# Indexed additions that wait once a head, four buffers for the activations on their way back, and attention steps placed ahead of the weight split

## The chip, the cores and the metric

The kernel is one program on 1 core of a Trainium2 chip. The metric is device time in microseconds (us): the median of several executions, lower is better. Engines are named as in the profile: PE is the matrix engine, DVE the vector engine, ACT the scalar engine, POOL the GpSimd engine, SP the engine whose queue loads the weights.

## The reference

The reference is a forward pass over 256 tokens of width 2048 in float32, in two blocks. Cut to what matters here:

```
# first block
proj  = rmsnorm(x) @ w_in                       # 2048 -> 6160
mixed = forgetting attention (16 heads) | dilated attention (16 heads)
h     = x + norm(mixed) @ w_out
q     = rmsnorm(h) @ w_query                    # 8 heads x 2 halves x 128
scores[h, half] = q @ sub_keys                  # 128 keys each
# per token and head: the best 16 of 16 x 16 sums -> 16 experts of 16384
gates   = softmax(best 16 sums)
h      += sum over (gates * gelu(expert_down[e] . x)) * expert_up[e]
# second block
proj  = rmsnorm(h) @ w_in_2                     # 2048 -> 5136
mixed = window attention (12 heads) | gated linear attention | stick-breaking attention (8 heads)
h    += norm(mixed) @ w_out_2
h    += relu(rmsnorm(h) @ w1)**2 @ w2           # 2048 -> 8192 -> 2048
out   = rmsnorm(h)
```

Within one head the 16 chosen experts of a token are 16 different ones. Two different heads can choose the same expert for one token; then their gates add up.

## The kernel before

**Weights.** Every large product goes through the weights in chunks of 256 rows by 512 columns (440 or 428 in the two `w_in` products), 8 chunks to a block of columns. For each chunk SP loads `raw`, ACT copies it to `w_hi` (line 558), DVE makes `w_lo = raw - w_hi` (line 563), and PE multiplies: 12 matmuls a chunk, high by high, high by low and low by high for two row tiles and two token tiles (lines 1618 to 1620, or 1769 to 1771 in the parts whose order is written out by hand). `raw`, `w_hi` and `w_lo` have 4 buffers each (`RING`), so ACT can start the split of chunk q when PE is through with chunk q-4.

**Order.** Each engine runs its own program, and semaphores join them. The programs of ACT, DVE and PE count the same chunks. Between chunks they carry the rest of the work at fixed positions: `SEQ` and `SEQ2` list the chunks of the two attention blocks, `PAIR_AT`, `SWA_AT` and `SB_AT` the chunk s = at behind which PE starts a pair of heads, and since splits run ahead, ACT and DVE have the matching step at s = at + `LEAD` (4) and later. Within a position of ACT or DVE the order is that of the text: the split of chunk s first, then the steps.

A pair of window heads on DVE and ACT: `copy_pair` (ACT, line 679), `max_swa` (DVE, lines 1463 to 1469), `exp_swa` (ACT, lines 917 to 919), `copy_swa_p` (DVE, line 1487), `out_swa` (DVE, line 1478). On PE: `turn_swa` (line 2024), the scores (line 2038), `turn_pair_p` (line 1739), `pv_swa`. The stick-breaking pairs have `copy_sb` (ACT, line 929), `sb_front`, `sb_logs` (line 1510), the addition, the weights (line 1577) and `sb_out` on DVE, and on PE the scores (line 2076), `sums_sb` (line 2087) and `pv_sb` (line 2100).

**The expert part.** All 16384 experts are computed for all tokens: 8 down rounds of 4 blocks make the hidden values, 8 up rounds multiply the gated hidden values by `expert_up`. A block's hidden values (512 experts by 256 tokens) are spilled by ACT to `hid_rows` in memory, and are brought back in the up rounds. In the first 4 down rounds DVE also searches the best 16 of each head (`search`); each of its 8 searches ends in line 1275 and releases 32 slots of one half of the tokens.

**The gates.** POOL adds each gate into a table in memory with an indexed DMA (`scatter`, line 466): one for each of the 128 slots of each of the two token halves, 256 in all, 128 elements each. A slot's addition waits until the one before it on the same table has landed:

```python
if slot:
    pool.wait_ge(added_gate[t], 16 * slot)
```

The two tables take turns, the second 16 slots behind the first. When both tables are complete, POOL loads a block's gates into `gat`, 2 buffers (line 530).

**The way back.** ACT's queue loads the hidden values of one block into `back`, one buffer (`reload`, line 771); PE transposes them (`turn_back`, line 1876); DVE multiplies by the gates (`fill`, line 1286); ACT and DVE split the product (`split_gated`, line 775; `rest`, line 1291). Four such blocks feed an up round. The steps lie at the last chunks of the block before it and the first chunks of its own first block: the first `fill` of all stands behind the split of chunk 5 of the last down block.

Of the kernel before, what the change touches and what calls it, by code (L numbers as in the profile page):

```python
# [26 lines left out]
P = 128  # L27
# [9 lines left out]
SUB = 8  # L37
# [126 lines left out]
def build(nc, a, out):  # L164

    ctx = ExitStack()
    with ctx:
# [45 lines left out]
        gat = big[:, 0:2048].rearrange("p (i t n) -> p i t n", i=2, t=NT)  # L213
# [96 lines left out]
        spilled, reloaded = sem("spilled"), sem("reloaded")  # L310
# [23 lines left out]
        gates_loaded = [sem(f"gates_loaded{i}") for i in range(2)]  # L334
# [110 lines left out]
        def _(pool):  # L445
# [16 lines left out]
            def scatter(t, slot):  # L462

                if slot:
                    pool.wait_ge(added_gate[t], 16 * slot)
                nc.gpsimd.indirect_dma_start(  # L466
                    tables[t], bass.IndirectOffsetOnAxis(ap=slot_at[:, t, slot:slot + 1].bitcast(U32), axis=0),
                    slot_gate[:, t, slot:slot + 1], None, compute_op=ALU.add).then_inc(added_gate[t], 16)
# [54 lines left out]
            for t in range(NT):  # L523
                pool.wait_ge(added_gate[t], 16 * P)
            for n in range(4 * PEER_ROUNDS):
                if n >= 2:
                    pool.wait_ge(hid_full, n - 1)
                for t in range(NT):
                    rows = tables[t].rearrange("(b p n) o -> b p (n o)", b=32, p=P)
                    pool.dma_start(gat[:, n % 2, t], rows[n]).then_inc(gates_loaded[n % 2], 16)  # L530
# [37 lines left out]
        def _(act):  # L568
# [134 lines left out]
            for s, (name, b, c) in enumerate(SEQ):  # L703
                if s == 15:
                    drain_in1(0)
                if s > 15 and s % SUB == 3 and s - 11 < 112:
                    drain_in1((s - 11) // SUB)
                if s in (157, 165, 173):
                    drain_query((s - 157) // SUB)
                split_hi(act, s // SUB, s % SUB, widths.get(name, WIDE))  # L710
                for j, at in enumerate(XTURN_AT):
                    if s == (j if j < 8 else at + LEAD):
                        x_hi_tiles(j)
                if 8 <= s < 12:
                    square_quarter(0, s - 8)
                if s == 13:
                    root(0)
                if s == 16:
                    act.wait_ge(fix_loaded, 16)
                    act.activation(ident_b[:], ident, ACT.Copy).then_inc(masks_made, 1)  # L720
                if s == 17:
                    act.wait_ge(rel_made, 1)
                    act.activation(relrow, ps[0:SWA_H, 6, 0:TW + 1], ACT.Copy).then_inc(row_copied, 1)
                if s == 22:
                    act.wait_ge(gate_abs, 1)
                    step(act.activation(fg[:, 2], fg[:, 1], ACT.Exp, scale=-1.0))
                    act.activation(fg[:, 3], fg[:, 2], ACT.Ln, bias=1.0).then_inc(gate_soft, 1)
                if s == 26:
                    act.wait_ge(cum_made, 1)
                    act.activation(c8, ps[0:16, 7, 0:S], ACT.Copy, scale=8.0).then_inc(cum_copied, 1)  # L730
                for n, at in enumerate(PAIR_AT):
                    if s == at + LEAD:
                        copy_pair(n)
                    if s == at + LEAD + 1:
                        exp_pair(n)
                if s in (94, 95):
                    square_half(1, s - 94)
                if s == 97:
# [28 lines left out]
            def reload(n):  # L767
                act.wait_ge(spilled, 16 * (n + 1))
                if not static(n) or n > 0:
                    act.wait_ge(hid_turned, n)  # L770
                act.dma_start(back[:].rearrange("p t n -> p (t n)"), hid_rows[n]).then_inc(reloaded, 16)

# [5 lines left out]
            def phase(up, nd, nu, prev_up, fill_next, extra=None, more=True):  # L778
                for i in range(4):
                    for c in range(SUB):  # L780
# [12 lines left out]
                        if i == 3 and fill_next:  # L793
                            f = 4 * (nu + 1 if up else nu)
                            if c == 5:
                                reload(f + 1)
                            if c == 6:
                                split_gated(f, (0, 4))
                            if c == 7:
                                reload(f + 2)  # L800
                        if i == 0 and up:
                            f = 4 * nu
                            if c == 0:
                                split_gated(f + 1, (1, 6))
                            if c == 1:
                                reload(f + 3)
                            if c == 2:
                                split_gated(f + 2, (2, 4))
                            if c == 3 and more:
                                reload(f + 4)  # L810
                            if c == 4:
                                split_gated(f + 3, (3, 6))
# [16 lines left out]
            def first_gates(pos):  # L829
                if pos == 20:  # L830
                    reload(0)

# [4 lines left out]
            phase(False, PEER_ROUNDS - 1, 0, False, True, first_gates)  # L837
# [21 lines left out]
            phase(True, 8, 7, True, False, open2, more=False)  # L859
# [78 lines left out]
            for s, (name, b, c) in enumerate(SEQ2):  # L938
                if s == 18:
                    drain_in2(0)  # L940
                if s >= 19 and s % SUB == 3 and s < 100:
                    drain_in2((s - 11) // SUB)
                split_hi(act, b2 + s // SUB, s % SUB, widths.get(name, WIDE))
# [20 lines left out]
                for n, at in enumerate(SWA_AT):  # L964
                    if s == at + LEAD:
                        copy_pair(PAIRS + n)
                    if s == at + LEAD + 1:
                        exp_swa(n)
                for n, at in enumerate(SB_AT):
                    if s == at + LEAD:  # L970
                        copy_sb(n)
# [29 lines left out]
        def _(dve):  # L1001
# [160 lines left out]
            for s, (name, b, c) in enumerate(SEQ):  # L1162
# [3 lines left out]
                split_lo(dve, s // SUB, s % SUB, widths.get(name, WIDE))  # L1166
                for n, at in enumerate(PAIR_AT):
                    if s == at + LEAD + 1:
                        max_pair(n)
                for j, at in enumerate(XTURN_AT):  # L1170
                    if s == (j if j < 8 else at + LEAD):
                        x_lo_tiles(j)
# [22 lines left out]
                for n, at in enumerate(PAIR_AT):  # L1195
                    if s == at + LEAD + 3:
                        copy_pair_p(n)
                    if s == at + LEAD + 5:
                        out_pair(n)
# [80 lines left out]
            def fill(f, g):  # L1280

                dve.wait_ge(gates_loaded[g % 2], 32 * (2 * f + g // 2 + 1))
# [3 lines left out]
                V.tensor_tensor(pair, pair, gat[:, g % 2].rearrange("p t (j s) -> p j t s", j=JJ), ALU.mult).then_inc(hid_full, 1)  # L1286
# [234 lines left out]
            for s, (name, b, c) in enumerate(SEQ2):  # L1521
# [44 lines left out]
                for n, at in enumerate(SWA_AT):  # L1566
                    if s == at + LEAD + 3:
                        copy_swa_p(n)
                    if s == at + LEAD + 5:
                        out_swa(n)  # L1570
                for n, at in enumerate(SB_AT):
                    if s == at + LEAD + 5:
                        dve.wait_ge(sb_sum, n + 1)
                        V.tensor_tensor(sbb, ps[:, 4:6, 0:3 * P], sbb, ALU.add).then_inc(sb_add, 1)
                    if s == at + LEAD + 7:
                        dve.wait_ge(sb_exp, n + 1)
                        V.tensor_tensor(diagonals(sbw), diagonals(sbw), strict, ALU.mult).then_inc(sb_w, 1)
                    if s == at + LEAD + 8:
                        sb_out(n)
# [26 lines left out]
        def _(pe):  # L1606
# [260 lines left out]
            def turn_back(n, g):  # L1867

                pe.wait_ge(reloaded, 16 * (n + 1))
# [4 lines left out]
                for jj in range(4):  # L1874
                    for t in range(NT):
                        last = pe.transpose(ps[:, 4 + 2 * (g % 2) + jj // 2, (jj % 2) * S + t * P:(jj % 2) * S + t * P + P],  # L1876
                                            back[:, t, jj * P:jj * P + P], ident)
                last.then_inc(hid_turned, 1)

            def phase(up, nd, nu, prev_up, fill_next, extra=None):  # L1880
                for i in range(4):
# [6 lines left out]
                    for c in range(SUB):  # L1888
# [3 lines left out]
                        if i == 3 and fill_next and c % 2:  # L1892
                            turn_back(4 * (nu + 1 if up else nu) + c // 2, c // 2)
# [305 lines left out]
```

## Time and profile before

| | us |
|---|---|
| median of 3 runs | 3235.41 |
| lowest, highest | 3235.39, 3250.27 |
| the profiled execution, its own time | 3242.3 |
| its span, first to last instruction | 3240.2 |

The profile is one execution. The span is what the trace covers; the execution's own time is 2.1 us longer. A group's "idle before" is the idle time of its engine just ahead of it, and the arrow names what ended it. Since matmuls are pipelined, the trace shows a busy PE also where each matmul only waits for the one before it to drain.

### The profile page before, as it was taken

What the parts mean: (1) busy time and instruction counts of PE and PEld (TensorE: products, weight loads), DVE (VectorE), ACT (ScalarE), POOL (GpSimd) and SP (SyncE); (2) the same over time, 40 slices, a digit from 0 to 9 for tenths busy, and PEclk for the clock granted to TensorE, in tenths of its full rate; (3) what the DMA queues carried; (4) which work ended last, traced back from release to release, by engine and by line L of the source; (5) the groups of instructions that cost most, each with busy time, mean ns of one, the idle gap of its engine ahead of it and who ended that gap; (6) DMA issues with size and microseconds to landing.
All of it is one profiled execution on the core that took longest, in us unless ns stands there. A gap on an engine that the chain in (4) does not pass through costs nothing.

```text
span 3240.2 us, 40579 instructions
## 1 busy us (share of the span) xinstructions
PE 3089.4 (95%) x14724; PEld 2614.1 (81%) x14724; DVE 1775.5 (55%) x2339; ACT 1465.0 (45%) x1822; POOL 584.5 (18%) x423
## 2 busy tenths in 40 slices
PE   8999999999999995299999999999889999999998
PEld 7988888888888884288888887899777888888886
DVE  5445564798844442255556555555657554545444
ACT  5445454555444442144344443554455544435453
POOL 3110000147777776300000000000000000000000
PEclk9999999999999998699999999999999999999999
DMA  6764467677777775477677776664345666666664
GB/s 213 241 200 133 129 215 258 183 218 210 223 223 215 215 220 124 123 227 221 217 231 235 237 233 220 188 204 136 109 126 152 192 191 189 188 193 184 191 187 151
DMA packets 215975, 627.60 MB, mean 194 GB/s; under 512 B 58139, under 2 KB 58789, under 8 KB 215472
## 3 DMA queue, kind: packets, MB, share of 16 engines
q1 hardware_dynamic: 156544, 549.79, 54.9%
q0 software_dynamic: 49856, 42.52, 6.1%
q10 hardware_dynamic: 9456, 33.71, 2.9%
q8 instruction: 73, 1.20, 0.2%
q14 instruction: 46, 0.38, 0.0%
HBM read 587.78 MB, written 38.14 MB: 193 GB/s over the span
## 4 chain that ended last, share of the span: by engine, by line
PE 70%; DMA 18%; POOL 4%; DVE 3%; issue 2%; ACT 2%; ACTq 0%; DVEq 0%; POOLq 0%
DMA gates<-srch 17%; PE ps L1620 14%; PE ps L1618 14%; PE ps L1619 14%; PE ps L1769 7%; PE ps L1771 7%; PE ps L1770 7%; POOL gates L466 4%; DMA back<-hid_rows 1%; DVE w_lo L563 1%; PE ps L1876 1%; ACT w_hi L558 1%; PE ps L1720 1%; PE ps L1633 0%; PE ps L1739 0%
## 5 line engine op out<-in xcount | busy, mean ns | idle before, releaser
L563 DVE TENSOR_TENSOR w_lo<-raw,w_hi 128x1024 fp32r<-128x1024 f32 (+2 forms) x1072 | 1281.3, 1198 | 1239.4 <-ACT w_hi L558 1236.5
L558 ACT ACTIVATE w_hi<-raw 128x1024 fp32r<-128x1024 f32 (+2 forms) x1072 | 1106.6, 1035 | 1412.9 <-PE ps L1620 1063.1
L1618 PE MATMUL ps<-w_hi,a_hi 128*128 128x512 f32 x1536 | 602.3, 392 | 0.0
L1620 PE MATMUL ps<-w_hi,a_lo 128*128 128x512 f32 x1536 | 598.6, 390 | 0.0
L1619 PE MATMUL ps<-w_lo,a_hi 128*128 128x512 f32 x1536 | 598.4, 390 | 0.0
L1618 PE MATMUL ps<-w_hi,x_hi 128*128 128x512 f32 x1504 | 587.7, 391 | 0.0
L1620 PE MATMUL ps<-w_hi,x_lo 128*128 128x512 f32 x1504 | 585.7, 389 | 0.0
L1619 PE MATMUL ps<-w_lo,x_hi 128*128 128x512 f32 x1504 | 585.4, 389 | 0.0
L466 POOL DMA_INDIRECT gates<-srch x256 | 482.2, 1884 | 297.5 <-DMA gates<-srch 204.9
L1769 PE MATMUL ps<-w_hi,x_hi 128*128 128x440 f32 (+2 forms) x1184 | 452.6, 382 | 3.0 <-DVE x_lo L1053 3.0
L1771 PE MATMUL ps<-w_hi,x_lo 128*128 128x440 f32 (+2 forms) x1184 | 439.9, 372 | 0.0
L1770 PE MATMUL ps<-w_lo,x_hi 128*128 128x440 f32 (+2 forms) x1184 | 439.8, 371 | 0.0
L1620 PEld LDWEIGHTS ps<-w_hi,a_lo 128*128 128x128 f32 x1536 | 288.7, 188 | 60.4
L1619 PEld LDWEIGHTS ps<-w_lo,a_hi 128*128 128x128 f32 x1536 | 288.9, 188 | 58.9
L1618 PEld LDWEIGHTS ps<-w_hi,a_hi 128*128 128x128 f32 x1536 | 288.8, 188 | 58.6
L1620 PEld LDWEIGHTS ps<-w_hi,x_lo 128*128 128x128 f32 x1504 | 282.4, 188 | 59.0
L1619 PEld LDWEIGHTS ps<-w_lo,x_hi 128*128 128x128 f32 x1504 | 282.6, 188 | 58.1
L1618 PEld LDWEIGHTS ps<-w_hi,x_hi 128*128 128x128 f32 x1504 | 282.6, 188 | 57.9
L1769 PEld LDWEIGHTS ps<-w_hi,x_hi 128*128 128x128 f32 x1184 | 225.2, 190 | 28.0 <-DVE x_lo L1053 3.9
L1771 PEld LDWEIGHTS ps<-w_hi,x_lo 128*128 128x128 f32 x1184 | 224.6, 190 | 22.5
L1770 PEld LDWEIGHTS ps<-w_lo,x_hi 128*128 128x128 f32 x1184 | 225.4, 190 | 20.5
L530 POOL DMA_DIRECT2D big<-gates x64 | 34.3, 541 | 616.7 <-DVE ps L1286 614.8
(335 smaller groups left out, 1681.2 us busy)
## 6 DMA issues: line engine op xcount, KB each, us to landing
raw<-in_peer_down SPq DMA_DIRECT2D x256, 512.0 KB, 3.8
raw<-in_peer_up SPq DMA_DIRECT2D x256, 512.0 KB, 4.2
raw<-in_w_mlp_in SPq DMA_DIRECT2D x128, 512.0 KB, 3.6
raw<-in_w_mlp_out SPq DMA_DIRECT2D x128, 512.0 KB, 3.6
raw<-in_w_in SPq DMA_DIRECT2D x112, 440.0 KB, 4.0
raw<-in_w_in SPq DMA_DIRECT2D x96, 428.0 KB, 3.2
raw<-in_w_out SPq DMA_DIRECT2D x64, 512.0 KB, 3.5
gates<-zero POOLq DMA_DIRECT2D x32, 512.0 KB, 4.9
```

What stands on the lines that cost most here:

```text
L466: nc.gpsimd.indirect_dma_start(tables[t], bass.IndirectOffsetOnAxis(ap=slot_at[:, t, slot:slot + 1].bitcast(U32), axis=0), slot_gate[:, t, ...
L530: pool.dma_start(gat[:, n % 2, t], rows[n]).then_inc(gates_loaded[n % 2], 16)
L558: act.activation(w_hi[:, c % RING, 0:2 * n], raw[:, c % RING, 0:2 * n], ACT.Copy).then_inc(hi_made, 1)
L563: nc.vector.tensor_tensor(w_lo[:, c % RING, 0:2 * n], raw[:, c % RING, 0:2 * n], w_hi[:, c % RING, 0:2 * n].bitcast(F32), ALU.subtract).th ...
L1618: mm(o, xh, wh, start=(k == 0), stop=False)
L1619: mm(o, xh, wl, start=False, stop=False)
L1620: last = mm(o, xl, wh, start=False, stop=(k == KT - 1))
L1720: mm(ps[:, 6 + j, at:at + w], qkT[at_, t * P:t * P + P], qkT[at_, S:S + w], start=True, stop=False)
L1769: mm(o, xh, wh, start=(c == first and kk == 0), stop=False)
L1770: mm(o, xh, wl, start=False, stop=False)
L1771: last = mm(o, xl, wh, start=False, stop=(c == last_c and kk == 1))
L1876: last = pe.transpose(ps[:, 4 + 2 * (g % 2) + jj // 2, (jj % 2) * S + t * P:(jj % 2) * S + t * P + P], back[:, t, jj * P:jj * P + P], ident)
```

## The change

1. **Additions.** `scatter` waits for its table only at slots 16, 32, ..., 112: once a head, for all additions of the heads before. Within a head the additions follow each other without a wait.
2. **The way back.** The hidden values come back through `hid_ring`, 4 buffers in columns of `big` that are free by then; `gat` has 4 buffers too. POOL issues both loads, block by block: the hidden values of block n when PE has transposed block n-4, the gates when DVE has filled block n-4. The first reload stands in POOL's order behind the last addition, the first gates behind the wait for both tables. ACT's `reload` and the single `back` are gone.
3. **Order in the attention blocks.** On ACT `copy_pair` and `copy_sb` stand ahead of the split of their position. On DVE the steps that feed PE stand ahead of the split: `max_pair`, `copy_pair_p`, `max_swa`, `copy_swa_p`, and all steps of the stick-breaking pairs. `exp_pair`, `exp_swa`, `out_pair` and `out_swa` stay behind it.

The additions and the way back, cut to the core, both on POOL:

```diff
-                if slot:
+                if slot and slot % TOPK == 0:
                     pool.wait_ge(added_gate[t], 16 * slot)
...
-            for t in range(NT):
-                pool.wait_ge(added_gate[t], 16 * P)
             for n in range(4 * PEER_ROUNDS):
-                if n >= 2:
-                    pool.wait_ge(hid_full, n - 1)
+                buf = n % RING
+                pool.wait_ge(spilled, 16 * (n + 1))
+                if n >= RING:
+                    pool.wait_ge(hid_turned, n - RING + 1)
+                pool.dma_start(hid_ring[:, buf].rearrange("p t n -> p (t n)"), hid_rows[n]).then_inc(reloaded[buf], 16)
+                if n == 0:
+                    for t in range(NT):
+                        pool.wait_ge(added_gate[t], 16 * P)
+                if n >= RING:
+                    pool.wait_ge(hid_full, n - RING + 1)
                 for t in range(NT):
                     rows = tables[t].rearrange("(b p n) o -> b p (n o)", b=32, p=P)
-                    pool.dma_start(gat[:, n % 2, t], rows[n]).then_inc(gates_loaded[n % 2], 16)
+                    pool.dma_start(gat[:, buf, t], rows[n]).then_inc(gates_loaded[buf], 16)
```

ACT, first attention block (the second likewise, with `SWA_AT` and `SB_AT`):

```diff
+                for n, at in enumerate(PAIR_AT):
+                    if s == at + LEAD:
+                        copy_pair(n)
                 split_hi(act, s // SUB, s % SUB, widths.get(name, WIDE))
...
                 for n, at in enumerate(PAIR_AT):
-                    if s == at + LEAD:
-                        copy_pair(n)
```

DVE, first attention block:

```diff
-                split_lo(dve, s // SUB, s % SUB, widths.get(name, WIDE))
                 for n, at in enumerate(PAIR_AT):
                     if s == at + LEAD + 1:
                         max_pair(n)
+                    if s == at + LEAD + 3:
+                        copy_pair_p(n)
+                split_lo(dve, s // SUB, s % SUB, widths.get(name, WIDE))
```

DVE, second attention block:

```diff
-                split_lo(dve, b2 + s // SUB, s % SUB, widths.get(name, WIDE))
                 for n, at in enumerate(SWA_AT):
                     if s == at + LEAD + 1:
                         max_swa(n)
+                    if s == at + LEAD + 3:
+                        copy_swa_p(n)
                 for n, at in enumerate(SB_AT):
                     if s == at + LEAD + 1:
                         sb_front(n)
                     if s == at + LEAD + 3:
                         sb_logs(n)
+                    if s == at + LEAD + 5:
+                        dve.wait_ge(sb_sum, n + 1)
+                        V.tensor_tensor(sbb, ps[:, 4:6, 0:3 * P], sbb, ALU.add).then_inc(sb_add, 1)
+                    if s == at + LEAD + 7:
+                        dve.wait_ge(sb_exp, n + 1)
+                        V.tensor_tensor(diagonals(sbw), diagonals(sbw), strict, ALU.mult).then_inc(sb_w, 1)
+                    if s == at + LEAD + 8:
+                        sb_out(n)
+                split_lo(dve, b2 + s // SUB, s % SUB, widths.get(name, WIDE))
```

## Rows read from the trace of the kernel before

**Rows 1.** The page, part 1: busy us, share of the span, instructions.

```profile
PE 3089.4 (95%) x14724; PEld 2614.1 (81%) x14724; DVE 1775.5 (55%) x2339; ACT 1465.0 (45%) x1822; POOL 584.5 (18%) x423
```

**Rows 2.** Waits of PE, whole span: us in total, times, longest.

```profile
PE ps L1876 <- DMA back<-hid_rows: 96.0, 8, 90.0
...
PE ps L1739 <- ACT hs L919: 5.9, 3, 3.1
PE ps L2024 <- DVE big L1487: 5.0, 3, 2.1
PE ps L2087 <- issue: 3.9, 1, 3.9
PE ps L2100 <- DVE k_end L1577: 3.9, 4, 1.2
PE ps L1739 <- DVE big L1478: 3.4, 1, 3.4
PE ps L2076 <- ACT big L929: 3.2, 3, 1.7
```

**Rows 3.** Timeline of PE, 1345 to 1366 us: start, duration, idle before.

```profile
1352.38 1.97 PE L1876 MATMUL ps<-fix,back 128*128 128x128 f32 x8 [90.03 <-DMA back<-hid_rows]
...
1362.22 1.09 PE L1876 MATMUL ps<-fix,back 128*128 128x128 f32 x8 [1.81 <-DMA back<-hid_rows]
```

**Rows 4.** Timeline of DVE, 1200 to 1420 us.

```profile
1250.78 1.23 DVE L563 TENSOR_TENSOR w_lo<-raw,w_hi 128x1024 fp32r<-128x1024 f32 x1 [1.40 <-ACT w_hi L558]
1347.35 1.23 DVE L1286 TENSOR_TENSOR ps<-ps,big 128x1024 f32<-128x1024 f32 x1 [95.35 <-DMA big<-gates]
```

**Rows 5.** Groups of POOL by line, 622 to 1252 us: busy, mean ns, idle.

```profile
L466 POOL DMA_INDIRECT gates<-srch x221 | 427.8, 1936 | 262.2 <-DMA gates<-srch 174.8 <-DVE srch L1275 60.4 <-issue 27.0
```

**Rows 6.** Timeline of POOL, 1100 to 1160 us.

```profile
1109.52 2.41 POOL L466 DMA_INDIRECT gates<-srch  x1 [0.30 <-issue]
...
1141.47 1.55 POOL L466 DMA_INDIRECT gates<-srch  x1 [0.31 <-issue]
```

**Rows 7.** Timeline of DVE, 1100 to 1160 us.

```profile
1109.27 1.23 DVE L563 TENSOR_TENSOR w_lo<-raw,w_hi 128x1024 fp32r<-128x1024 f32 x1 [1.49 <-ACT w_hi L558]
...
1141.91 1.23 DVE L563 TENSOR_TENSOR w_lo<-raw,w_hi 128x1024 fp32r<-128x1024 f32 x1 [1.04 <-ACT w_hi L558]
```

**Rows 8.** Timeline of POOL, 1250 to 1350 us.

```profile
1287.83 1.55 POOL L466 DMA_INDIRECT gates<-srch  x1 [0.31 <-issue]
...
1340.10 1.55 POOL L466 DMA_INDIRECT gates<-srch  x1 [1.71 <-DMA gates<-srch]
```

**Rows 9.** Line 563 on DVE, 622 to 1252 us: ns min/median/max.

```profile
L563 DVE TENSOR_TENSOR w_lo<-raw,w_hi x232: 1216/1226/1280, 622.5 to 1250.8; 128x1024 fp32r<-128x1024 f32 x116
```

**Rows 10.** Line 466 on POOL, 1050 to 1255 us, issue to landing.

```profile
DMA to landing us min/median/max: 3.5/4.9/6.3
```

**Rows 11.** The page, part 6: issues, KB, median us to landing.

```profile
raw<-in_peer_down SPq DMA_DIRECT2D x256, 512.0 KB, 3.8
back<-hid_rows ACTq DMA_DIRECT2D x32, 512.0 KB, 5.0
big<-gates POOLq DMA_DIRECT2D x64, 256.0 KB, 4.2
```

**Rows 12.** Busy time, granted clock, DMA share and GB/s by stretch.

```profile
1050.00:1250.00 200.00, 200.00 (x887) 165.65 (x886) 89.81 (x74) 89.44 (x93) 146.70 (x75) 1.00 0.80 221
1354.00:1366.00 12.00, 10.19 (x47) 8.22 (x46) 8.49 (x8) 5.48 (x7) 1.65 (x5) 0.94 1.00 380
2320.00:2400.00 80.00, 67.77 (x363) 62.42 (x362) 52.96 (x75) 36.48 (x75) 0.00 (x0) 0.89 0.37 113
```

**Rows 13.** Timeline of DVE, 2255 to 2330 us.

```profile
2268.81 1.05 DVE L563 TENSOR_TENSOR w_lo<-raw,w_hi 128x856 fp32r<-128x856 f32 x1 [1.71 <-ACT w_hi L558]
...
2277.66 1.05 DVE L563 TENSOR_TENSOR w_lo<-raw,w_hi 128x856 fp32r<-128x856 f32 x1 [0.45 <-ACT w_hi L558]
2278.62 0.95 DVE L1487 COPY big<-ps 128x768 f32<-128x768 f32 x1
```

More of the change, by code:

```diff
@@ L212, in build @@
         sc = big[:, 10240:14336].rearrange("p (t g n) -> p t g n", t=NT, g=16)
-        gat = big[:, 0:2048].rearrange("p (i t n) -> p i t n", i=2, t=NT)
+        gat = big[:, 0:4096].rearrange("p (i t n) -> p i t n", i=RING, t=NT)
+        hid_ring = big[:, 4096:8192].rearrange("p (i t n) -> p i t n", i=RING, t=NT)
         hid = big[:, 17184:18208].rearrange("p (t n) -> p t n", t=NT)
@@ L309, in build @@
         hid_hi, hid_lo = sem("hid_hi"), sem("hid_lo")
-        spilled, reloaded = sem("spilled"), sem("reloaded")
+        spilled = sem("spilled")
+        reloaded = [sem(f"reloaded{i}") for i in range(RING)]
         fix_loaded, kc_loaded = sem("fix_loaded"), sem("kc_loaded")
@@ L333, in build @@
         added_gate = [sem(f"added_gate{t}") for t in range(NT)]
-        gates_loaded = [sem(f"gates_loaded{i}") for i in range(2)]
+        gates_loaded = [sem(f"gates_loaded{i}") for i in range(RING)]
         bl_turned, bl_copied, gpre_made = sem("bl_turned"), sem("bl_copied"), sem("gpre_made")
@@ L765, in spill @@
                 act.dma_start(hid_rows[n], hid.rearrange("p t n -> p (t n)")).then_inc(spilled, 16)
[L767 to L771, printed above, removed]
             def split_gated(n, pair):
@@ L776, in split_gated, with phase @@
                                ps[:, pair[1]:pair[1] + 2, :].rearrange("p b n -> p (b n)"), ACT.Copy).then_inc(hid_hi, 1)
-            def phase(up, nd, nu, prev_up, fill_next, extra=None, more=True):
+            def phase(up, nd, nu, prev_up, fill_next, extra=None):
                 for i in range(4):
@@ L794, in phase @@
                             f = 4 * (nu + 1 if up else nu)
-                            if c == 5:
-                                reload(f + 1)
                             if c == 6:
                                 split_gated(f, (0, 4))
-                            if c == 7:
-                                reload(f + 2)
                         if i == 0 and up:
@@ L804, in phase @@
                                 split_gated(f + 1, (1, 6))
-                            if c == 1:
-                                reload(f + 3)
                             if c == 2:
                                 split_gated(f + 2, (2, 4))
-                            if c == 3 and more:
-                                reload(f + 4)
                             if c == 4:
@@ L827, in beside @@
                 return extra
-            def first_gates(pos):
-                if pos == 20:
-                    reload(0)
             for r in range(4):
@@ L836, in _ @@
                 phase(False, r, 0, False, False)
-            phase(False, PEER_ROUNDS - 1, 0, False, True, first_gates)
+            phase(False, PEER_ROUNDS - 1, 0, False, True)
             phase(True, PEER_ROUNDS, 0, False, True)
@@ L858, in _ @@
             act.wait_ge(gT_made, 2)
-            phase(True, 8, 7, True, False, open2, more=False)
+            phase(True, 8, 7, True, False, open2)
             def gla(pos):
@@ L942, in _ @@
                     drain_in2((s - 11) // SUB)
+                for n, at in enumerate(SWA_AT):
+                    if s == at + LEAD:
+                        copy_pair(PAIRS + n)
+                for n, at in enumerate(SB_AT):
+                    if s == at + LEAD:
+                        copy_sb(n)
                 split_hi(act, b2 + s // SUB, s % SUB, widths.get(name, WIDE))
@@ L964, in _ @@
                 for n, at in enumerate(SWA_AT):
-                    if s == at + LEAD:
-                        copy_pair(PAIRS + n)
                     if s == at + LEAD + 1:
@@ L969, in _ @@
                 for n, at in enumerate(SB_AT):
-                    if s == at + LEAD:
-                        copy_sb(n)
                     if s == at + LEAD + 2:
@@ L1195, in _ @@
                 for n, at in enumerate(PAIR_AT):
-                    if s == at + LEAD + 3:
-                        copy_pair_p(n)
                     if s == at + LEAD + 5:
@@ L1280, in fill @@
             def fill(f, g):
-                dve.wait_ge(gates_loaded[g % 2], 32 * (2 * f + g // 2 + 1))
+                dve.wait_ge(gates_loaded[g], 32 * (f + 1))
                 dve.wait_ge(hid_turned, 4 * f + g + 1)
@@ L1285, in fill @@
                 pair = pair.rearrange("p (j t s) -> p j t s", j=JJ, t=NT)
-                V.tensor_tensor(pair, pair, gat[:, g % 2].rearrange("p t (j s) -> p j t s", j=JJ), ALU.mult).then_inc(hid_full, 1)
+                V.tensor_tensor(pair, pair, gat[:, g].rearrange("p t (j s) -> p j t s", j=JJ), ALU.mult).then_inc(hid_full, 1)
             def rest(n, g):
@@ L1566, in _ @@
                 for n, at in enumerate(SWA_AT):
-                    if s == at + LEAD + 3:
-                        copy_swa_p(n)
                     if s == at + LEAD + 5:
                         out_swa(n)
[L1571 to L1579, printed above, removed]
                 if s == 99:
@@ L1865, in key_scores, with turn_back @@
                 last.then_inc(sc_made, 1)
-            def turn_back(n, g):
-                pe.wait_ge(reloaded, 16 * (n + 1))
+            def turn_back(f, g):
+                n = 4 * f + g
+                pe.wait_ge(reloaded[g], 16 * (f + 1))
                 if not static(n) or n >= 2:
@@ L1876, in turn_back @@
                         last = pe.transpose(ps[:, 4 + 2 * (g % 2) + jj // 2, (jj % 2) * S + t * P:(jj % 2) * S + t * P + P],
-                                            back[:, t, jj * P:jj * P + P], ident)
+                                            hid_ring[:, g, t, jj * P:jj * P + P], ident)
                 last.then_inc(hid_turned, 1)
@@ L1892, in phase @@
                         if i == 3 and fill_next and c % 2:
-                            turn_back(4 * (nu + 1 if up else nu) + c // 2, c // 2)
+                            turn_back(nu + 1 if up else nu, c // 2)
                         if extra:
```

## The prediction

> **What bounds the kernel now.** I read the busy shares first. PE is busy for 3089.4 us of the 3240.2 us span, 95%, and no other engine for more than 55% [rows 1]. So a change can only win where PE stands still. The list of PE's waits says where that is: 96.0 us in 8 waits on the hidden values coming back, of which one wait is 90.0 us long [rows 2]. Six more groups, 25.3 us together, are waits on ACT or DVE in the second attention block; the releasers named there (lines 919, 1478, 1487, 1577, 929, and one that the profile calls issue) belong to its window and stick-breaking pairs.
>
> The 90.03 us wait ends at 1352.38, so it began at 1262.35 [rows 3]. The list blames the reload. The timeline of DVE shows more: after the split at 1250.78 DVE stood for 95.35 us, until the first `fill` at 1347.35, released by the gates [rows 4]. The reload of block 2 comes behind that fill in ACT's order, so the reload is only the last link. What was late is the gates, and they were late because of the additions: the last one was issued at 1340.10, and the fill followed 7.25 us later [rows 8, 4].
>
> **Part 1, the additions.** From 622 to 1252 us POOL issued 221 additions: 427.8 us busy (1.94 each), 174.8 us waiting for an earlier one to land, 27.0 us of issue [rows 5]. The waits are what the change removes. What remains per addition is its own duration and a gap of 0.30. Undisturbed it lasts 1.55, so 1.86 with the gap [rows 8].
>
> The duration depends on DVE's split. The addition at 1109.52 starts 0.25 us into the split of 1109.27 and lasts 2.41; the one at 1141.47 lasts 1.55, although the split of 1141.91 starts in the middle of it and takes its normal 1.23 [rows 6, 7]. So only the first instant of an addition is held by a running split, until that split ends; then it needs 1.42 more. Without waits an addition follows directly on the other, and in a stretch of regular chunks the two can lock: one addition per chunk period of 1.23 + 1.49 = 2.72 [rows 7]. Bounds for the pace are thus 1.86 and 2.72. With today's durations it is 1.94 + 0.30 = 2.24.
>
> I choose between them by laying the 256 additions one behind the other over the starts of the 232 splits between 622.5 and 1250.8 [rows 9], each held as just described. The chain is knocked out of the lock about once a block, where the splits shift, and the mean hold becomes 0.46 us: 256 x (1.86 + 0.46) = 594 us. The 14 waits that are left, one for each head and table, add some 13 us, because an addition takes 4.9 us to land under load [rows 10] and the other table's turn covers only half of that. The last addition is then issued at 622.3 + 607 = 1230, a mean pace of 2.37. As a test, the same laying-out with today's waits, and landings 2.9 us after an addition's end, puts the last one at 1341; the trace has 1340.10.
>
> When must it be issued? The fill can start at 1252.0, when the split of 1250.78 ends. From last addition to fill are 7.25 us in the quiet stretch; under load the landing takes some 2 us longer, so 1242.8. That leaves 13 us, or a pace up to 2.42. Another 7 us or so are free behind that, because PE had split chunks until 1262.35. So I take the whole 90.0 us as gone. The granted clock comes back with it: the first transposes after the stall took 1.97 instead of 1.09 us [rows 3], and over the next 12 us the clock was 0.94 [rows 12], 0.9 + 0.7 = 1.6 us.
>
> A page of the Trainium skill speaks against this. "SBUF — State Buffer", section "SBUF: two separate sides", says that DVE and GpSimd take a shared port pair as an exclusive lock for a whole instruction, and that the other one fully blocks. By that rule addition and split would alternate, 1.55 + 1.23 = 2.78 us a pair. The trace agrees only in part: the hold is there, but a split that starts 0.44 us into an addition is not held at all [rows 6, 7]. The same outcome without the page is the first rival below.
>
> **Part 2, the way back.** The other 7 waits on the reload, 96.0 - 90.0 = 6.0 us, go: with four buffers a block's load is issued a whole round ahead, and it takes 5.0 us [rows 11]. What is new is a burst: behind the last addition POOL issues four blocks, 4 x (512 + 2 x 256) KB = 4 MB. The queues moved 221 GB/s at a share of 0.80 then and reached 380 at 1.00 [rows 12], so 159 GB/s are spare and the burst lasts 26 us. The first fill needs only its first quarter, and 13 us are in hand. I cost it at nothing. The other end: the weights at half rate for 26 us, 13 us of PE. POOL's queue has nothing else to do in the up rounds, and ACT is spared 32 issues that no one waited for except through the reload.
>
> **Part 3, the order.** In the first attention block no group of PE's waits names a moved step, so I cost it at nothing. In the second, a moved step starts earlier by up to the split that stood before it, 1.05 us. Line 1487 ran at 2278.62 behind the split of 2277.66, ahead of which DVE had idled 0.45; it can go there, 1.0 to 1.5 us earlier [rows 13]. Three such waits, 5.0 us in all, give 3.5. The four of line 1577 are at most 1.2 each; the step no longer stands behind a split that itself waits for ACT: 3.9. The three of line 929 give 2.5 of 3.2, the three of line 919 give 2 of 5.9 (the scores come hardly before the 1.05 us split of 2268.81 ends), the sums at line 2087 give 1.1 of 3.9. Line 1478 is not moved: nothing. That is 13.0; I take 12. The clock was 0.89 over 80 us [rows 12], 8.8 us lost at most; I take a third, 3. Together 15. The ends are 0, if the engine's next step becomes the late one, and 25.3 + 8.8 = 34. A loss is possible too and has its own rival.
>
> **Sum.** Own time of the profiled execution 3242.3 - 90.0 - 6.0 - 1.6 - 15 = 3129.7, say 3130. The median of the runs was 3235.4, 7 us less. I do not subtract these 7: the runs differ most likely in how long the additions took, and that length no longer counts. If they differ elsewhere, 3123.
>
> **Rivals.**
> *The additions lock to the splits.* Each takes 2.72 throughout. By 1262 there are 235 out; with DVE at rest the last 21 go at 1.86, the last at 1301, the fill at 1309, 39 us earlier than now: 3242.3 - 39 - 6.0 - 15 = 3182. For it: the addition of 1109.52 shows the lock. Against: the durations, 1.94 in the mean, and the block edges.
> *The transfers are the limit.* If the memory side served the additions one after another, removing POOL's wait would only move the wait into the queue; the gates come no earlier and the change does not do what it says: 3242.3 - 6.0 - 15 = 3221. For it: landing takes 4.9 us under load. Against: at 1287.83 an addition was issued 1.86 us after the one before [rows 8], which had not landed, and the stretch before the stall had two tables at work at 221 GB/s without PE waiting for weights [rows 12].
> *The moved steps starve PE (slower).* A split now waits for a step, and the step for PE. Splits run three chunks ahead, some 7 us, and ACT and DVE take one each of about 1 us, so some 5 us are free. If every one of the 26 pairs overruns that by 5 us, it costs 130 us: 3242.3 - 97.6 + 130 = 3275. It decides from 4.1 us a pair on. Against: DVE is busy only 53 of 80 us there [rows 12], so it can catch up between the steps.
>
> **Chances.** The forecast 0.83, the lock 0.10, the transfers 0.04, starved PE 0.03. The forecast's own range goes from 3104 (all 34 us of part 3, and the 7 us between the runs) to 3170 (part 3 nothing, the burst 13, a pace of 2.5 us, which ends at 1262 and costs some 12 us). It leaves out 0.17 for the rivals, and is my range. About 0.5%, 16 us, is what a measurement of this kernel can tell from no change. Faster: forecast and lock, 0.93. Same: the transfers, 14 us below, 0.04. Slower: 0.03.
>
> **What will show it.** Right: additions with gaps of 0.30 and waits on a landing at most 14 times; the last one issued near 1220 to 1240; no wait of PE over 3 us on line 1876, and the clock at 1.00 there; PE's waits in the second attention block near 12 us. The lock shows as durations near 2.4 and a last issue near 1300; the transfers as landing times growing past 10 us; starved PE as waits of lines 1769 to 1771 on `w_lo` of line 563. The prediction is wrong first where the pace passes 2.42 us.

## The result, and the profile after

The changed kernel takes 3112.95 us in the median of 4 runs (3111.83 to 3113.9), against 3236.52 of before in the same count; the ratio is 0.9609, 95% interval 0.9583 to 0.9635. The forecast was 3130 with a range of 3104 to 3170. The profiled execution has a span of 3110.0 us, 130.2 less than before.

The waits of PE over the whole span, the view of [rows 2], for the changed kernel:

```profile
...
PE ps L1731 <- DVE big L1471: 4.4, 1, 4.4
PE ps L2080 <- issue: 3.0, 1, 3.0
PE ps L1761 <- DVE x_lo L1046: 2.4, 2, 1.3
PE ps L1731 <- ACT hs L910: 2.3, 1, 2.3
PE ps L1962 <- DVE big L1363: 1.2, 1, 1.2
PE ps L1935 <- DVE x_lo L1338: 0.8, 1, 0.8
PE ps L2017 <- DVE big L1480: 0.5, 1, 0.5
```

The line numbers have moved by a few (1876 is 1869 now, 466 is 468, 563 is 571, 1286 is 1279, 1478 is 1471). No wait on the transposes of line 1869 is left. Of the attention waits, 1731 on line 910 fell from 5.9 to 2.3, 2017 from 5.0 to 0.5, 2080 on "issue" from 3.9 to 3.0, and the groups of the old lines 2100 (3.9) and 2076 (3.2) are gone. One grew, 1731 on line 1471, from 3.4 to 4.4.

The group of the additions on POOL, whole span: busy us, mean ns, idle before, and what ended it; then the timeline of POOL at the end of the additions.

```profile
L468 POOL DMA_INDIRECT gates<-srch x256 | 518.4, 2025 | 151.3 <-issue 77.5 <-DVE srch L1268 61.4 <-DMA gates<-srch 12.5
```

```profile
1215.55 2.41 POOL L468 DMA_INDIRECT gates<-srch  x1 [0.30 <-issue]
1218.27 1.56 POOL L468 DMA_INDIRECT gates<-srch  x1 [0.30 <-issue]
...
1224.53 1.59 POOL L468 DMA_INDIRECT gates<-srch  x1 [0.30 <-issue]
1225.55 1.18 POOL L530 DMA_DIRECT2D big<-hid_rows  x1
1229.88 1.14 POOL L538 DMA_DIRECT2D big<-gates  x2 [3.15 <-DMA gates<-srch]
```

The rows show the lock of one addition per chunk period, 2.72 us from start to start, and its end at a block edge (1218.27). Over the whole span the mean duration rose from 1.88 us (482.2 us for the same 256 additions before) to 2.03 us, while the waits on landings fell from 204.9 us to 12.5 in all. The last addition is issued at 1224.53. Behind it come the first reload and, after 3.15 us of waiting for the last addition to land, the first gates.

The timeline of DVE where it had stood for 95.35 us [rows 4]:

```profile
1245.23 1.23 DVE L571 TENSOR_TENSOR w_lo<-raw,w_hi 128x1024 fp32r<-128x1024 f32 x1 [1.40 <-ACT w_hi L566]
1246.38 1.23 DVE L1279 TENSOR_TENSOR ps<-ps,big 128x1024 f32<-128x1024 f32 x1
```

Busy time in one stretch, the columns of [rows 12] (PE, PEld, DVE, ACT, POOL, then clock, DMA share, GB/s):

```profile
1235.00:1275.00 40.00, 40.00 (x194) 33.44 (x194) 25.47 (x22) 20.12 (x22) 7.14 (x14) 1.00 1.01 388
```

The first fill (line 1279, at 1246.38) now follows the split ahead of it without a wait. The burst of loads is there, 388 GB/s at a full share for 40 us and more, and PE is busy through it at full clock.

**Where the 130.2 us came from.** The starts of four operations cut the spans into stages that hold the same work: the last step of the first search (line 1275, now 1268), the first transposes of hidden values, and the first and last transposes of the residual behind the expert part (line 1942, now 1935).

| stage | before | after | less |
|---|---|---|---|
| start to the end of the first search | 621.3 | 615.8 | 5.5 |
| to the first transposes of hidden values | 628.1 | 628.1 | 0.0 |
| to the first transposes behind the experts (2035.6, now 1928.2) | 786.2 | 684.3 | 101.9 |
| to the last of these transposes (2527.5, now 2397.4) | 491.9 | 469.2 | 22.7 |
| to the end | 712.7 | 712.6 | 0.1 |

### The profile page after: what moved, and what is told of

Its sections match the earlier page's. It is cut to its first block and busy times, and to the rows that moved or that the text cites. A ratio compares the mean times of both kernels' runs of the same rounds, so it can differ in the third digit from the quotient of the medians.

```text
span 3110.0 us, 40502 instructions
## 1 busy us (share of the span) xinstructions
PE 3073.7 (99%) x14724; PEld 2609.2 (84%) x14724; DVE 1773.8 (57%) x2339; ACT 1464.2 (47%) x1822; POOL 638.3 (21%) x455
## 5 line engine op out<-in xcount | busy, mean ns | idle before, releaser
L468 POOL DMA_INDIRECT gates<-srch x256 | 518.4, 2025 | 151.3 <-issue 77.5
L530 POOL DMA_DIRECT2D big<-hid_rows x32 | 17.7, 555 | 475.0 <-PE ps L1869 471.6
```

Source lines behind the costliest of these rows:

```text
L468: nc.gpsimd.indirect_dma_start(tables[t], bass.IndirectOffsetOnAxis(ap=slot_at[:, t, slot:slot + 1].bitcast(U32), axis=0), slot_gate[:, t, ...
L530: pool.dma_start(hid_ring[:, buf].rearrange("p t n -> p (t n)"), hid_rows[n]).then_inc(reloaded[buf], 16)
```

## The experiments

They were run in three sets. The kernel before, run beside them, had medians of 3243.93, 3247.17 and 3247.95 (3235.19 to 3259.44), 7 to 11 us more than above. The changed kernel shows no such shift: two kernels whose edits left its time as it was, `e8_other_split` and `e10_out_first`, took 3113.94 and 3114.03 in the later sets.

### The three parts alone, and the change without the third

`e1_additions` is the kernel before with only this edit:

```diff
-                if slot:
+                if slot and slot % TOPK == 0:
```

> Part 1 alone on the kernel before: additions wait once a head, the way back and the order as before. If the late gates made the 90 us stall: 3242 - 90 - 5 (clock) = 3147, the last addition issued near 1230, the seven short waits on the reload still there (6 us). If the single reload buffer has a share in the stall: part of the 90 us stays, over 3170. If additions were limited by the transfers: 3230 or more.

Measured: 3151.51 (3142.8 to 3160.51), ratio 0.9703, interval 0.9664 to 0.9741, that is 92.4 less than the 3243.93 beside it. PE's waits on the transposes:

```profile
PE ps L1876 <- DMA back<-hid_rows: 4.9, 5, 3.0
```

They are 4.9 us in 5 waits, the longest 3.0. So this one condition removes the stall, and the single reload buffer had no share in it. The last addition is issued at 1234.5. The runs differ by 18 us. In the two slower ones the granted clock over the whole run is 0.993, in the two faster ones 0.996. `e5_every_4` below, in whose profile PE stood, has 0.992 to 0.995. Whether PE stood in the two slower runs here, no trace shows.

`e2_way_back` has only the four buffers and POOL's loads, `e3_order` only the new order.

```diff
+                pool.dma_start(hid_ring[:, buf].rearrange("p t n -> p (t n)"), hid_rows[n]).then_inc(reloaded[buf], 16)
+                if n == 0:
+                    for t in range(NT):
+                        pool.wait_ge(added_gate[t], 16 * P)
...
-                act.dma_start(back[:].rearrange("p t n -> p (t n)"), hid_rows[n]).then_inc(reloaded, 16)
```

> Part 2 alone on the kernel before: four buffers for hidden values and gates, loaded by POOL, the additions still one by one. If the reload is only the last link of the stall: its 6 us of short waits go and the long wait stays within a few us of 90, about 3232. If the reload chain made the stall: below 3170.

Measured: 3239.1 (3227.62 to 3245.86), ratio 0.9973, interval 0.9952 to 0.9995. It is 4.8 us less in the medians; but its wait is not one within a few us of 90:

```profile
1356.57 1.97 PE L1867 MATMUL ps<-fix,big 128*128 128x128 f32 x8 [102.63 <-DMA big<-hid_rows]
```

The timeline of PE shows one wait of 102.63 us, begun at 1253.94, at the very first transposes. Before, PE did the first two sets of transposes and stood from 1262.35 [rows 3]. The new order of POOL's queue puts the first reload behind the last addition, so PE stops one link earlier. It also goes on sooner: 5.6 us after the last addition (1350.96), where before it took 12.3 us, since the reload that PE waited for there stood behind the fill. So the longer wait does not make the kernel longer.

```diff
+                for n, at in enumerate(PAIR_AT):
+                    if s == at + LEAD:
+                        copy_pair(n)
                 split_hi(act, s // SUB, s % SUB, widths.get(name, WIDE))
```

> Part 3 alone on the kernel before. By the stage times of the two traces (first attention block 3.6 to 5.5 us shorter, window pairs 11.4, stick-breaking pairs 11.3): 26 to 28 us less, about 3210, and the stall stays. By the prediction's term: 15 us less, about 3222. Rival, that part of these stages' gain comes from the other two parts: under 20 us less.

Measured: 3221.88 (3214.11 to 3231.38), ratio 0.9919, interval 0.9888 to 0.9951. 22 us less, between the two figures expected. The interval, 16 to 36 us, holds the 26 to 28 and just leaves out the 15.

`e4_no_order` has the first two parts and the old order.

> Parts 1 and 2 without part 3: the changed kernel with the old order in the attention blocks. If the parts add up: 3113 + 27 = 3140. By the prediction's term of 15 us: 3128. The down rounds and up rounds as in the changed kernel, no wait over 0.5 us on the transposes of the hidden values.

Measured: 3138.87 (3135.65 to 3142.95), ratio 0.9657, interval 0.9627 to 0.9688. Against 3112.95 the order is worth 25.9 us, close to the 27 by which the parts would add up and far from the 15 of the prediction. This kernel has no wait at all on the transposes of hidden values. Against `e1_additions` the way back is worth 12.6 between the medians, with the 18 us of spread in that kernel; alone, in `e2_way_back`, it brought 4.8.

### Where the gain of the order comes from

`e6_act_order` is the changed kernel with only ACT's moves, `e7_dve_order` with only DVE's, `e12_second_only` with both engines' moves in the second attention block only. For DVE's part of the first block, left out in `e6_act_order` and `e12_second_only`:

```diff
+                split_lo(dve, s // SUB, s % SUB, widths.get(name, WIDE))
                 for n, at in enumerate(PAIR_AT):
                     if s == at + LEAD + 1:
                         max_pair(n)
-                    if s == at + LEAD + 3:
-                        copy_pair_p(n)
-                split_lo(dve, s // SUB, s % SUB, widths.get(name, WIDE))
...
                 for n, at in enumerate(PAIR_AT):
+                    if s == at + LEAD + 3:
+                        copy_pair_p(n)
                     if s == at + LEAD + 5:
                         out_pair(n)
```

> The changed kernel with only ACT's steps moved ahead of the split, DVE's as before. If DVE's order brings most of the 26 us (its splits of 1.05 us stood before the late steps): 3133 to 3136, PE's waits on line 929 of before (3.2 us) gone, those on the window and stick-breaking steps of DVE left. Rival, ACT's order brings half: 3126.

Measured: 3139.2 (3136.58 to 3141.17), as without any order, and more than the 3133 to 3136 expected. PE's waits in the second attention block tell why:

```profile
PE ps L2094 <- DVE k_end L1570: 8.1, 4, 3.0
```

The 3.2 us on ACT's copy went, and the four waits for the weights of the stick-breaking pairs (old line 2100) grew from 3.9 to 8.1. That fits a PE that came to them earlier while DVE was no faster.

> The changed kernel with only DVE's steps moved. If DVE's order brings most: 3115 to 3119. Rival, ACT's order brings half: 3126. If the two help only together: both this and the kernel with ACT's alone stay above 3130.

Measured: 3116.83 (3115.36 to 3118.36), 22 us of the 26. The three waits on ACT's copy, 3.2 us in its profile, are most of the difference that is left to 3112.95. ACT's move is worth 4 us, and only where DVE's has been made.

> The changed kernel with the new order in the second attention block only, the first as before. By the prediction the first block's order is worth nothing: 3113. By the stage times of the two profiles it is worth 3.6 to 5.5 us: 3117 to 3118.

Measured: 3117.71 (3116.43 to 3118.59). The first block's order is worth 4.8 us. In its profile the first search ends at 621.0, as before (621.3); in the changed kernel at 615.8. One profile each would not settle that, since this end varies by some us between executions, but the 14 profiles agree: it lies between 615.8 and 619.3 in the eight kernels with the new order on DVE in this block, and between 620.9 and 625.6 in the six with the old.

The same stages as above, from the profiles (us):

| stage | before | `e1_additions` | `e4_no_order` | `e12_second_only` | changed |
|---|---|---|---|---|---|
| to the end of the first search | 621.3 | 621.1 | 625.6 | 621.0 | 615.8 |
| to the first transposes of hidden values | 628.1 | 628.1 | 628.1 | 628.1 | 628.1 |
| to the first transposes behind the experts | 786.2 | 694.4 | 684.3 | 684.3 | 684.3 |
| to the last of these transposes | 491.9 | 487.9 | 488.0 | 469.0 | 469.2 |
| to the end | 712.7 | 712.7 | 712.7 | 712.7 | 712.6 |

### How much slack the additions have

`e5_every_4` makes the changed kernel wait four times as often.

```diff
-                if slot and slot % TOPK == 0:
+                if slot and slot % 4 == 0:
```

> The changed kernel with a wait before every 4th addition of a table instead of every 16th. The laying-out over the split starts of the changed kernel, with landings 3.0 us after an addition's end, gives 40 to 45 waits and the last addition at 1261 to 1267 (with 16: 1223 to 1227). The first fill, which could start at 1246.4, then starts near 1272; PE has work for some 10 us more, so it stands some 16 us: 3113 + 17 = 3130. If the 13 us in hand were an error and the additions had no slack: 3113 + 38 = 3151. If the waits don't set the end of the additions: 3113.

Measured: 3135.55 (3127.57 to 3142.18), and 3142.18 in the profiled run, the slowest of the four. It is 5.5 us more than the 3130 expected. The timeline of POOL shows the last addition, that of DVE the first fill, that of PE the wait:

```profile
1266.22 1.55 POOL L468 DMA_INDIRECT gates<-srch  x1 [0.30 <-issue]
```

```profile
1274.49 1.23 DVE L1279 TENSOR_TENSOR ps<-ps,big 128x1024 f32<-128x1024 f32 x1 [24.47 <-DMA big<-gates]
```

```profile
1271.81 1.97 PE L1869 MATMUL ps<-fix,big 128*128 128x128 f32 x8 [24.20 <-DMA big<-hid_rows]
```

The laying-out gave 1261 to 1267 for the last addition, and 1266.2 it was. But PE stood 24.2 us and not 16: it stopped at the first transposes, at 1247.6, with work split in front of it. PE went on 5.6 us after the last addition, before the fill. The link was the reload.

`e9_reload_first`, the kernel of `e5_every_4` with the four loads ahead of the wait for the tables, was meant to test that. Of its edit this part is new:

```diff
+            for n in range(RING):
+                pool.wait_ge(spilled, 16 * (n + 1))
+                pool.dma_start(hid_ring[:, n].rearrange("p t n -> p (t n)"), hid_rows[n]).then_inc(reloaded[n], 16)
             for t in range(NT):
                 pool.wait_ge(added_gate[t], 16 * P)
```

> The kernel with a wait before every 4th addition, and the first four loads of hidden values ahead of the wait for both tables instead of between the gates' loads. In the kernel with every 4th, PE stood 24.2 us at the first transposes, whose load POOL issues behind the last addition. If that load is the link: PE now transposes on time, works until its split chunks are used up, and stands only from about 16 us after that to some 4 us behind the first fill, 16 us less 0 to 2: 8 to 10 us less in the profile, about 3127 in the median. If the gates alone were the link, nothing changes: 3136.

Measured: 3132.67 (3130.28 to 3134.33), 2.9 less, between the two figures expected. The edit missed its aim: the loads still stand behind the last addition in POOL's order, and the first of them stood there before. The profile has PE's wait at the first transposes again, 14.85 us until 1262.25, 6.5 us after the last addition at 1255.8. It is shorter because the additions ended 10 us earlier in this execution. So it says nothing against the link and does not test it further; loads put among the additions, which would, were not run.

### What holds an addition

`e8_other_split` gives DVE's split to another operation on the same operands.

```diff
-            nc.vector.tensor_tensor(w_lo[:, c % RING, 0:2 * n], raw[:, c % RING, 0:2 * n],
-                                    w_hi[:, c % RING, 0:2 * n].bitcast(F32), ALU.subtract).then_inc(lo_made, 1)
+            nc.vector.scalar_tensor_tensor(out=w_lo[:, c % RING, 0:2 * n], in0=raw[:, c % RING, 0:2 * n], scalar=1.0,
+                                           in1=w_hi[:, c % RING, 0:2 * n].bitcast(F32), op0=ALU.mult,
+                                           op1=ALU.subtract).then_inc(lo_made, 1)
```

> The changed kernel with every split on DVE done by another operation (scalar 1.0 times raw, minus w_hi) on the same operands. If any DVE operation with two inputs from SBUF holds an addition: durations of 2.41 stay and the last addition is issued near 1224. If the hold belongs to the plain subtraction: additions last 1.55 throughout, the last near 1112. The time stays 3113 either way, since the additions have slack, if the operation takes the same 1.23 us; if it takes 0.2 us longer it is still hidden behind PE.

Measured: 3113.94 (3112.91 to 3114.74), the same time. Timeline of DVE, then of POOL:

```profile
1195.27 1.23 DVE L571 SCALAR_TENSOR_TENSOR w_lo<-raw,w_hi 128x1024 fp32r<-128x1024 f32 x1 [1.49 <-ACT w_hi L566]
```

```profile
1195.51 2.42 POOL L468 DMA_INDIRECT gates<-srch  x1 [0.30 <-issue]
```

The hold stays, 2.42 us for an addition that starts 0.24 us into the split, and the last addition is at 1226.2. Both operations read two inputs from SBUF. In the changed kernel's profile one more kind of operation with two such inputs, the comparison of line 1217 (128x512), held additions, by up to 0.41 us; operations of the search with one input held none by more than 0.02.

### Two attempts at a faster version

`e10_out_first` puts `out_swa` ahead of the gated attention's step of its position, `e11_exp_first` also ACT's exponentials ahead of ACT's split.

```diff
+                for n, at in enumerate(SWA_AT):
+                    if s == at + LEAD + 5:
+                        out_swa(n)
                 if 32 <= s < 96:
                     gla(s - 32)
```

> The changed kernel with the last step of a window pair (line 1471) ahead of the gated attention's step of the same position, which is a reciprocal of 4.94 us once. If that reciprocal makes the 4.4 us wait of PE on line 1471: the wait goes, 3113 - 4.4 - 1 to 2 for the clock = 3107 to 3109. If PE then waits for the next step behind the reciprocal (line 1480): 3111 or more.

Measured: 3114.03 (3112.31 to 3115.24), no gain. The 4.4 us wait is gone, but one other has grown from 2.3 and a new one has come:

```profile
PE ps L1731 <- ACT hs L910: 3.1, 1, 3.1
...
PE ps L2041 <- DVE big L1480: 1.7, 1, 1.7
```

The reciprocal of 4.94 us is only pushed back by 0.8 us. It still stands ahead of the copy of line 1480 and of the next pair's steps, and now these are late.

> As the kernel before it in this list, and ACT's exponentials of a window pair ahead of the split of their position. If ACT's split of 0.9 us still stands before them: the 2.3 us wait on line 910 falls by up to 0.9, 3106 to 3108. Rival: ACT waits for the maxima with its split undone, no gain or a loss of 1 to 3 us.

Measured: 3127.38 (3125.59 to 3131.27), 14 us more. The loss is larger than the 1 to 3 us of the rival. PE waits 7.7 us in three waits on line 1471, the step that stands behind DVE's split. The timeline of ACT shows the first of a pair's exponentials:

```profile
2213.42 0.40 ACT L908 ACTIVATE big<-biased,hs 128x128 f32<-128x128 f32 x1 [5.45 <-DVE hs L1462]
```

ACT stood for 5.45 us until DVE had the maxima, with its split of that position undone. DVE's split waits for ACT's, so it and everything behind it came later. No version that was run beats the changed kernel.

## Why the prediction was right, and where it was off

**The bound** was read rightly: the list of waits named the reload, the stall was the additions'. `e1_additions` shows it, 92 us for one condition. In its profile the stage of the experts is 91.8 us shorter than before, where the prediction had 90.0 + 1.6.

**The pace of the additions** was the step that decided, and it held: 594 us for 256 durations and gaps plus 13 us of waits were expected, 607 in all; the trace has 616.8 to 1224.5, 607.7, of which 12.5 are waits on landings. That it agrees to a microsecond is luck: in the eight other profiles with the same waits it is 603.3 to 612.4. The same laying-out gave the end of `e5_every_4` (1266.2, for 1261 to 1267), but `e9_reload_first`, with the same additions, issued the last one at 1255.8. So the laying-out is good to some 10 us there. The rival in which every addition locks (3182) falls with the mean duration of 2.03 us, the rival of the transfers (3221) with the 12.5 us of waits.

The page "SBUF — State Buffer" of the Trainium skill, section "SBUF: two separate sides", counts a DVE operation with two SBUF inputs among those that lock out a GpSimd operation that reads SBUF; `e8_other_split` agrees, for two operations, with 2.41 and 2.42 us. The lock over the whole instruction does not show: additions and splits would have to alternate, and a split that starts in the middle of an addition keeps its 1.23 us [rows 6, 7].

**The stall's term**, 90.0 + 6.0 + 1.6 = 97.6, measured 101.9 in the stage of the experts. `e1_additions` splits this: the additions brought 91.8, for 90.0 + 1.6, and from 694.4 to 684.3 the way back brought 10.1, for 6.0. All eight profiles with four buffers and no stall have 684.3 in this stage. So the term that was too small is the way back's. Of the 10.1 us, 4.9 are PE's waits on the reload in `e1_additions`. Behind the longest, 2.96 us, the clock was 0.83 from 1910 to 1920 us, 1.7 us lost. (The kernel before has the same behind a wait of 2.55 us, 0.83 from 2000 to 2010 us.) Such a loss I had not counted. The other 3.5 us are spread over the transposes, and I can't place them.

**The slack** was stated wrongly in one place. "Another 7 us or so are free behind that" holds for the old order, where the reload of block 0 was long done. In the changed kernel that reload stands behind the last addition, and PE stops at its first transposes: 102.63 us instead of 90.03 in `e2_way_back`, 24.2 instead of 16 in `e5_every_4`. It cost nothing here because the additions ended in time: the first transposes came at 1243.9, and 1224.5 + 5.6 = 1230.1 was early enough.

**The order of the attention blocks** was the term that was mis-sized: 15 us expected, 28.2 in the stages and 25.9 between the medians. One step of it failed outright: "no group of PE's waits names a moved step, so I cost it at nothing". In the first block the order is worth 4.8 us (`e12_second_only`). In the second block the stage is 22.7 us shorter than before, for 15. The waits there fell from 28.3 us (the 25.3 of [rows 2] and two groups of 1.8 and 1.2) to 12.2, by 16 instead of 12. I had counted 3 for the clock. Here is the same stretch of work before, then without the order (`e4_no_order`), then in the changed kernel:

```profile
2275.00:2400.00 125.00, 107.72 (x592) 98.68 (x590) 77.69 (x117) 60.29 (x123) 0.00 (x0) 0.92 0.39 118
2177.40:2302.40 125.00, 106.13 (x605) 96.79 (x603) 79.00 (x119) 64.12 (x128) 0.00 (x0) 0.96 0.40 120
2167.60:2292.60 125.00, 113.98 (x652) 103.89 (x651) 86.81 (x133) 70.76 (x138) 0.00 (x0) 0.96 0.43 130
```

The clock was 0.92 before and is 0.96 now, but it is 0.96 without the order as well. There the stage takes 488.0, and 487.7 to 488.7 in the three other profiles of the new runs with the old order on DVE. So some 4 of the 22.7 us go with the lower clock of the one execution before, and the order itself is worth 18.8 in this stage (21.2 between the medians of `e4_no_order` and `e12_second_only`). Of these 18.8, 16 are waits that are gone. The other 3 are neither in PE's waits nor in the clock, and stay open. The rival of a starved PE (3275) does not show on DVE's side; `e11_exp_first` shows that it is real once a moved step waits long, 13 us against `e10_out_first` for the six window pairs.

**The burst** lasts longer than the 26 us expected, since POOL goes on with the next blocks as buffers come free, and no cost of it shows: PE is busy for all of the 40 us.

**The base.** I began from the profiled execution's 3242.3, 7 us above the median, since the additions' length would make the runs differ. The changed kernel indeed varies by only 2 us. But `e1_additions`, with the same additions, varies by 18, so that is not the whole reason. It stays open which it is. Against the measured 3112.95 the forecast was 17 us high. By the stages of the profiles that is 13 from the order, of which some 4 are the clock of the one execution before, and 4 from the way back.

## What to carry to other kernels

When a wait names a transfer, follow the order of the queue that issued it: here the last link was a reload, the cause 256 additions that waited for each other, and one condition was worth 92 us. To price a queue's pace, lay its instructions over the other engine's timeline, holds included; the mean duration of a run full of waits is not that of one without. A step moved ahead of another pays only where its input is ready by then and the engine behind it keeps up: the same kind of move brought 22 us on DVE, 0 on ACT alone, 4 on ACT beside it, and cost 13 with ACT's exponentials.

## What the runs showed of the hardware

An indexed addition takes 1.55 us of POOL, and up to 2.59 when it starts within a DVE split, whichever of two operations makes the split; only its start is held. Among the operations of the search only one held it by more than 0.1 us in the changed kernel's profile, the comparison of line 1217, by up to 0.41. The mean pace was 2.37 us. The trace of before has 3.5 to 6.3 us from issue to landing [rows 10], so by an estimate some two additions were in flight at a time. The last one had landed within 5.35 us, and the waits on landings, 12.5 us in all, show that the queue behind POOL was not the limit.
